# Second layer's modulation sums in the first eight merge steps without gaps, in place of ten steps with two gaps

## The reference

```
for l in range(2):
    mod = silu(c) @ w_mod[l] + b_mod[l]          # 6*1024 values: sh1 sc1 g1 sh2 sc2 g2
    h = rmsnorm(x, norm1[l]) * (1 + sc1) + sh1
    q, k, v of three attention branches, gate_l = split(h @ w_in[l])
    o_a, o_b, o_n = three attentions
    y = sum over n of sigmoid(gate_l[n]) * (o_n @ w_branch[l, n])
    x = x + g1 * (y @ w_out[l])
    x = x + g2 * moe(rmsnorm(x, norm2[l]) * (1 + sc2) + sh2)     # 16 experts, top 2
return rmsnorm(x, final_norm)
```

## Time and profile before

| what | value |
|---|---|
| median of three executions | 1568.55 us (1566.22 to 1569.42) |
| profiled execution | 1573.06 us |
| its span from first to last instruction | 1571.4 us |
| TensorE busy | 1508.7 us, 96% of the span |
| VectorE busy | 743.1 us, 47% |
| merge of the second layer | about 1154 to 1268 us of the span |

### The profile page before, as it was taken

The page is one execution under the profiler, slowest core; times in us unless marked ns, Lnnn a source line. Parts: engine busy times, 40 slices in busy tenths (PEclk is TensorE's granted clock), DMA queues, the critical chain, the costliest instruction groups (busy, mean ns, idle before and its releaser), DMA issues. The chain is left out here.

```text
span 1571.4 us, 19180 instructions
## 1 busy us (share of the span) xinstructions
PE 1508.7 (96%) x7346; PEld 850.9 (54%) x7346; DVE 743.1 (47%) x1554; ACT 377.7 (24%) x908; POOL 144.7 (9%) x233
## 2 busy tenths in 40 slices
PE   8999999999999999999999989999999999989897
PEld 4478766666676646644433334456677655333332
DVE  2366278789995435511111245306788837111113
ACT  3022288811111111101111123106821111000001
POOL 0100001200000100001021220000300011111110
PEclk9999999999999998999999999999999997999899
DMA  9823230125744472589999996342149867999996
GB/s 332 275 54 108 73 132 5 38 77 140 273 154 167 157 308 100 188 300 376 391 417 420 393 343 203 137 175 90 42 115 369 314 249 278 384 406 412 409 376 284
DMA packets 110187, 371.89 MB, mean 237 GB/s; under 512 B 25616, under 2 KB 29856, under 8 KB 93540
## 3 DMA queue, kind: packets, MB, share of 16 engines
q1 hardware_dynamic: 96688, 332.42, 57.0%
q0 software_dynamic: 12976, 37.95, 6.8%
q10 hardware_dynamic: 432, 0.29, 0.1%
HBM read 363.20 MB, written 19.73 MB: 244 GB/s over the span
## 5 line engine op out<-in xcount | busy, mean ns | idle before, releaser
L2946 PE MATMUL bank<-ring_sb,HT_sb 128*64 128x512 f32 x544 | 122.9, 605 | 1.8 <-DMA ring_sb<-w_e_up 1.1
L2543 PE MATMUL bank<-ring_sb,HT_sb 128*128 128x512 f32 x256 | 114.9, 605 | 2.5 <-ACT HT_sb L1146 2.5
L1541 DVE SCALAR_TENSOR_TENSOR MB_sb<-ring_sb,cT_sb,MB_sb 128x512 f32<-128x512 f32 x144 | 108.2, 752 | 5.1
L2983 PE MATMUL bank<-ring_sb,QR_sb 128*64 128x512 f32 x336 | 80.9, 625 | 16.6 <-DMA ring_sb<-w_e_down 14.1
L2229 DVE TENSOR_TENSOR QR_sb<-QR_sb,bank 64x512 f32<-64x512 f32 x21 | 21.9, 1045 | 139.8 <-ACT QR_sb L1431 139.8
L2652 PE MATMUL bank<-QR_sb,ring_sb 128*128 128x512 f32 x192 | 86.3, 592 | 0.0
L2543 PEld LDWEIGHTS bank<-ring_sb,HT_sb 128*128 128x128 f32 x256 | 48.9, 194 | 63.1 <-issue 63.1
L2946 PEld LDWEIGHTS bank<-ring_sb,HT_sb 128*64 128x64 f32 x544 | 39.1, 139 | 74.2 <-issue 73.0
L2666 PEld LDWEIGHTS bank<-tab_sb,MB_sb 128*128 128x128 f32 x480 | 51.3, 141 | 44.6 <-issue 41.6
L2695 PE MATMUL bank<-KR_sb,QR_sb 64*128 64x512 f32 (+1 forms) x288 | 70.5, 568 | 3.9 <-ACT MB_sb L1348 2.9
L2666 PE MATMUL bank<-tab_sb,MB_sb 128*128 128x128 f32 x480 | 68.5, 280 | 1.7 <-DVE MB_sb L1880 1.4
(11 more groups left out here) (459 smaller groups left out, 2571.4 us busy)
## 6 DMA issues: line engine op xcount, KB each, us to landing
ring_sb<-w_e_down SPq DMA_DIRECT2D x32, 2048.0 KB, 18.3
ring_sb<-w_mod SPq DMA_DIRECT2D x24, 2048.0 KB, 9.9
ring_sb<-w_in SPq DMA_DIRECT2D x21, 2048.0 KB, 13.5
ring_sb<-w_e_gate SPq DMA_DIRECT2D x16, 2048.0 KB, 13.0
ring_sb<-w_e_up SPq DMA_DIRECT2D x16, 2048.0 KB, 17.2
ring_sb<-w_e_gate SPq DMA_DIRECT2D x22, 1024.0 KB, 16.5
ring_sb<-w_e_up SPq DMA_DIRECT2D x22, 1024.0 KB, 18.7
ring_sb<-w_branch SPq DMA_DIRECT2D x8, 1024.0 KB, 12.0
```

The source lines that it names most:

```text
L1541: link(stt(a, WR[slot][:, k], cT[:, k, strm:strm + 1], a, ALU.mult, ALU.add))
L2543: ins = mm(bank[j % 4][:, :], HT[:, k, P * t:P * t + P], WR[slot][:, k], start=(k == 0), stop=(k == KD - 1))
L2946: ins = mm(bank[0][HALF * side:HALF * side + HALF, :], hgT[q % 2][:, k, 0:HALF], w[k], start=(k == 0), stop=(k == KD - 1))
L2983: ins = mm(bank[4][HALF * half:HALF * half + HALF, :], eaT[:, k, 0:HALF], w[k][:, CW * half:CW * half + CW], start=(k == 0), stop=(k == 3))
```

## The change

`mod_step` returns i for both layers. For the second layer, the passes 0 to 7 counted for the steps 0, 1, 2, 4, 5, 6, 8, 9 before, and count for 0 to 7 now.

```
 def mod_step(l, i):
-    return i + i // 3 if l else i
+    return i
```

## The result

The changed kernel is slower: 1.0048 times the time of the kernel before, with a 95% interval of 1.003 to 1.0065. On the median of 1568.55 us that is 7.5 us (4.7 to 10.2), or 1576.1 us; the forecast was 4.9 us and 1573.4.

A forecast was written before the change was run, and what follows sets the result against it. TensorE was taken to bound the kernel, busy 96% of the span, with VectorE's joins nearly late in the merge. A 5.3 us loss in the merge less 0.4 behind it gave +4.9, or 1573.4 us; range 1567.5 to 1577.

The forecast's parts named there:

- The direction and the place: Second layer's merge: slower by 5.3 us, through TensorE's waits at steps 4, 6 and 8.
- g10's landing: Load queue, second layer's merge: M8 ahead of g10 delays its landing by 5.4 us, to 1191.2.
- The later issue of g10: Load queue: g10, issued after the pass over M6, costs nothing more, as wb1 still has some six us to move.
- VectorE's 41.1 us: VectorE in the merge: nonstop work from g10's landing to the join of step 6 takes 41.1 us.
- the 2.47: Merge: from the beginning of VectorE's join to the TensorE P1 it frees pass 2.47 us.
- the two pairs behind: TensorE at the merge's end: both last pairs of steps run at 19.03 us each, 38.06 together.
- The blocks and the stores: Merge: M9, M10, M11 and g11 land in time, and the store for step 6's rows causes no wait.
- Behind the merge: After the second layer's merge: VectorE's 7.99 us wait goes, TensorE saw 0.48 of it; gain 0.4 us.
- The experts: Experts' DMA-heavy stage: neither hides nor adds anything, shifts with TensorE.
- The clock: TensorE after step 4's 2.8 us wait: price between 0 and 2.7 us, taken as 0; chance of a fall 0.12.
- No later landing: Rival, merge: g10 lands as early as before, merge ends as before at 1267.5, time 1568.2 us; chance 0.21.
- nothing replaces the stalls: Rival, merge: VectorE's passes never hold a join, gain 2.0 us in the merge, time 1566.2 us; chance 0.05.

The follow-up runs named there:

- short passes: Changed kernel, but each second-layer pass adds up five of its eight slices; one execution only, no ratio, merge end 2.1 us later than before from step 2.
- old passes and new loads: Kernel before, but with the ring's loads in the order and slots of the changed kernel (M7, M8, wb1, g10); ratio 1.0167.
- new passes and old loads: Changed kernel, but with the ring's loads in the order and slots of the kernel before (M7, wb1, g10, M8); ratio 1.0025.
- M11 early: Changed kernel with the load order of the kernel before, except M11 moved ahead of wb2; ratio 0.9992.
- nine steps and gates first: Kernel before, with one pass in each of steps 0 to 7 and loads ordered by when they are wanted, g10 first; ratio 0.9990.

## Why the prediction held, point by point

- **The direction and the place** held: M8 ahead of g10 in the queue, VectorE without a stop behind it, TensorE's waits at steps 4, 6 and 8. Moving that one load back takes the merge's loss from 7.0 to 0.85 us, with every pass where the change put it.
- **g10's landing** was the term that was mis-sized. I had 5.4 us; it was 7.0 (24.4 against 17.4). One block was right in size: with short passes it is 31.25 - 25.69 = 5.6 us. The later issue of g10, taken to cost nothing, does not explain the rest: with old passes and new loads g10 was issued as late as in the changed kernel (18.3 us behind M7) and landed 30.8 us behind it, earlier than with short passes, where it was issued at 13.6. What failed is the step that only M8's block is added, since landings follow one another: the loads landed in the order of issue, but bytes of loads behind g10 moved before it was in. From M7's issue to g10's landing the DMA queue moved 9.78 MB in the changed kernel, of which the four blocks up to g10 are 8.39; before it moved 7.13, of which three blocks are 6.29. That is 1.39 MB of later loads against 0.84, and the difference is 1.4 us at 387 GB/s, with the engines full throughout. With short passes it was 0.80 MB, with old passes and new loads none. Why more of them came through here is not shown; and in the five kernels that have the old order up to M8, g10's landing itself lies between 23.9 and 25.7 us behind M7's issue, so one execution of each kernel does not make the 1.4 us firm.
- **VectorE's 41.1 us** from g10 to the join of step 6 were 41.41, the 2.47 from there to TensorE 2.46, and the two pairs behind 37.98 against 38.06. The blocks and the stores were in time as worked out. Together with the landing: 5.3 expected, 7.0 measured. TensorE's timeline adds up to the same: the waits of 4.31, 0.97, 0.41 and 1.29 and 1.7 us of slower clock at step 4, less the 1.56 and 0.21 that went, are 6.9.
- **Behind the merge** I had a gain of 0.4. TensorE's 0.48 went, as worked out; the stretch is 1.7 us shorter, most of it in the routing's small matmuls and the waits between them. In the four runs with new passes and g10 in time it is 48.4 to 49.2 us. But with short passes, the one other run with both the passes and the loads of the change, it is 47.4, close to the 47.3 here; so the rest may belong to the change, by a way that is not shown. As it is, the merge lost 1.7 us more than forecast and the stretch behind it gained 1.3 more: the two misses nearly cancel, and in part it is luck that the time came as near as it did.
- **The experts** shifted with TensorE: from the first expert to the end the kernels here take 251.2 to 254.2 us, 254.0 the changed one, with no order in it.
- **The clock.** I took no price. The clock did fall at step 4 (7.12 us for the 24 matmuls, against 5.42, behind a wait of 4.31), but the pair of step 6 waited for VectorE in any case (0.97), so that 1.7 us lay in VectorE's shadow. At step 8 waits of 0.41 and 1.29 left the clock alone. So the zero held for the sum, but the clock did fall. In the run with new passes and old loads the fall was paid for in full: 2.7 us. The Trainium skill, "TensorE: Matmul & The Clock Gate", section "Why this matters for your kernels", warns of idle gaps between bursts of matmuls, but of longer ones than the 2.14 and 1.28 us there, or the 2.34 us with short passes, behind which the clock fell; and behind 3.41 us, at step 4 with old passes and new loads, it did not fall (8 matmuls in 1.97 us). The measurements decide.
- **The rivals.** No later landing is shown false by the 24.4; had it been so, the prediction gave the merge as long as before, and the run with M11 early measured that, 0.1 us more. That nothing replaces the stalls did not come true with these loads; with nine steps and gates first TensorE waits at no head of a pair.

## What to carry to other kernels

If a number that spaces out work also feeds a planner of loads, look first at what the loads do: the same change of passes cost nothing that could be measured (1.0008) or 7.5 us, by where one 2 MB block stood in an in-order queue that was full. A load should stand in the queue by when its first reader wants it, here VectorE's sums two steps ahead of TensorE's step, not by the step for which it counts. An idle time ahead of a full queue is not slack that more bytes can fill.

## What the runs showed of the hardware

- TensorE fell to the lower clock level behind waits far shorter than the 6.45 us from which I had the price: behind two of 2.14 and 1.28 us with 1.04 us of work between them (granted 0.50, 24 matmuls in 8.16 us for 5.42), and in part behind one of 2.34 us (7.23 us for the same matmuls). Behind 0.43 and 1.28, or 1.03 and 1.29, it did not (5.42), and neither behind one of 3.41 us (old passes, new loads, step 4). So the length of one wait alone does not say whether the clock falls.
- In an in-order issue queue the delay of one load fed itself: g10's sums came 5 us later, counted from the beginning of the pair of step 2, and the merge ended 20.8 us later, because each load waited for a pass that waited for a load.
- Loads landed in the order of issue, and yet loads behind the one that was waited for took a share of the DMA engines before it landed: 1.39 MB in the changed kernel, 0.84 MB before.
